# A two-layer decoder trunk on one core: the program's opening reordered, the attention bias read from a repeated distance table, the first norm weights spread by matmuls

## What is computed

```python
y = xf * lax.rsqrt(jnp.mean(xf * xf, axis=-1, keepdims=True) + EPS)
h = y * norm_mix[layer]                       # (256, 1024)
proj = h @ w_in[layer]                        # the first columns: q, k, v of the DeltaNet, then 4 + 4 for beta and alpha
# attention of group gi with dilation dil, for query qi and key kj of a block
dist = qi + C_BLOCK - kj
bias = table[t5_bucket(jnp.maximum(dist, 0) * dil)]      # 32 x 12 table, one column per head and group
s = jnp.einsum('brhnqd,brhnkd->brhnqk', qb, kb) * (D ** -0.5) + bias
s = jnp.where(valid, s, -jnp.inf)
```

## Time and profile before

| | |
|---|---|
| runs | median 2117.56 us of 3 (2116.93 to 2118.57) |
| profiled execution | 2120.26 us, its span 2118.5 us |
| granted TensorE clock, mean over the span | 0.987 |
| busy share of the span | PE 96%, PEld 82%, DVE 76%, ACT 58%, POOL 1% |
| moved by DMA | 517 MB, 244 GB/s over the span |

### The profile page before, as it was taken

How to read it: one execution, slowest core, us unless ns; L and a number is a source line. 1 busy time by engine, 2 the same in 40 slices (tenths; PEclk the granted TensorE clock), 3 DMA queues, 4 the chain that set the end, 5 groups by cost and what they waited for, 6 DMA issues and landing times.

```text
span 2118.5 us, 28922 instructions
## 1 busy us (share of the span) xinstructions
PE 2027.8 (96%) x10759; PEld 1728.0 (82%) x10759; DVE 1609.6 (76%) x1256; ACT 1233.7 (58%) x1013; POOL 16.5 (1%) x22
## 2 busy tenths in 40 slices
PE   7999999989997999999979999999999999999997
PEld 6998888879997988888868878888887888888885
DVE  5878865755445878955766888898888889888985
ACT  4544455444433554455446777777777777777774
POOL 0000000000000000000000000000000000000000
PEclk9999999999999999999988999999999999999999
DMA  8523455245554522455247999999999999999994
GB/s 279 160 80 100 140 178 179 89 151 188 179 190 136 177 82 90 145 164 186 91 149 260 387 344 378 359 362 368 353 379 341 382 358 364 375 341 372 351 375 179
DMA packets 240481, 516.97 MB, mean 244 GB/s; under 512 B 11519, under 2 KB 34167, under 8 KB 240412
## 3 DMA queue, kind: packets, MB, share of 16 engines
q1 hardware_dynamic: 238124, 507.60, 68.1%
q0 software_dynamic: 2288, 8.41, 1.1%
HBM read 513.86 MB, written 2.12 MB: 244 GB/s over the span
## 4 chain that ended last, share of the span: by engine, by line
PE 87%; DVE 7%; ACT 3%; issue 2%; DMA 0%; SPq 0%; DVEq 0%; ACTq 0%
PE PS L476 25%; PE PS L478 25%; PE PS L477 25%; PE PS L547 7%; DVE lo L1533 2%; ACT hi L1102 2%; PE PS L1002 1%; PE PS L978 1%; PE PS L496 1%; PE PS L758 0%; DVE a_act L1634 0%; DMA rows<-in_knorm_c 0%; PE PS L948 0%; PE PS L789 0%; DVE t_n L1556 0%
## 5 line engine op out<-in xcount | busy, mean ns | idle before, releaser
L1533 DVE TENSOR_TENSOR lo<-raw,hi 128x2048 fp32r<-128x2048 f32 x481 | 1095.0, 2290 | 295.0 <-ACT hi L1102 292.3
L1102 ACT ACTIVATE hi<-raw 128x2048 fp32r<-128x2048 f32 x481 | 919.6, 1915 | 337.8 <-PE PS L478 330.5
L476 PE MATMUL PS<-hi,e_hi 128*128 128x512 f32 x896 | 355.3, 397 | 1.4 <-DVE e_lo L1556 1.4
L478 PE MATMUL PS<-hi,e_lo 128*128 128x512 f32 x896 | 350.2, 391 | 0.0
L477 PE MATMUL PS<-lo,e_hi 128*128 128x512 f32 x896 | 350.2, 391 | 0.0
L476 PE MATMUL PS<-hi,actT_hi 128*128 128x512 f32 x640 | 253.9, 397 | 4.6 <-DVE lo L1533 4.1
L478 PE MATMUL PS<-hi,actT_lo 128*128 128x512 f32 x640 | 249.6, 390 | 0.0
L477 PE MATMUL PS<-lo,actT_hi 128*128 128x512 f32 x640 | 249.1, 389 | 0.0
L476 PE MATMUL PS<-hi,fT_hi 128*128 128x512 f32 x536 | 210.6, 393 | 9.8 <-DVE fT_lo L1556 9.3
L477 PE MATMUL PS<-lo,fT_hi 128*128 128x512 f32 x536 | 209.5, 391 | 0.0
L478 PE MATMUL PS<-hi,fT_lo 128*128 128x512 f32 x536 | 209.3, 390 | 0.0
(11 more groups left out here) (323 smaller groups left out, 2153.8 us busy)
## 6 DMA issues: line engine op xcount, KB each, us to landing
raw<-in_moe_w SPq DMA_DIRECT2D x336, 1024.0 KB, 5.8
raw<-in_w_in SPq DMA_DIRECT2D x92, 1024.0 KB, 5.2
raw<-in_ffn_w SPq DMA_DIRECT2D x33, 1024.0 KB, 5.3
raw<-in_w_br SPq DMA_DIRECT2D x12, 1024.0 KB, 5.0
raw<-in_w_out SPq DMA_DIRECT2D x8, 1024.0 KB, 5.2
hankel<-hankel_dram POOLq DMA_DIRECT2D x1, 1536.0 KB, 13.6
x<-in_x SPq DMA_DIRECT2D x2, 512.0 KB, 4.0
gain<-in_norm_mix POOLq DMA_DIRECT2D x2, 512.0 KB, 5.8
```

What stands on the lines that cost most here:

```text
L476: pe.matmul(out, a_hi, b_hi, start=first, stop=False, skip_group_check=True)
L478: return pe.matmul(out, a_lo, b_hi, start=False, stop=last, skip_group_check=True)
L1102: act.activation(hi[prog.u % SPLIT][:, :], raw[slot][:, :], COPY).then_inc(hi_made.sem, 1)
L1533: dve.tensor_tensor(lo[prog.u % RAW][:, :], raw[prog.u % RAW][:, :], hi[s][:, :].bitcast(F32), ALU.subtract).then_inc(lo_made.sem, 1)
```

## The change

It has these parts.

- **SP and ACT queues.** SP issues one row of `norm_mix` (4 KB) to partition 0 of `gain`, x in two halves with a semaphore each, the identity alone, and the first two weight units; then the narrow weights, the two parameters, the other ten mask tiles, and the rest of the weights. The bucket table, the bias table and the six rows are issued by ACT as its first instructions. POOL's load of `gain` for layer 0 is gone.
- **PE's opening.** 22 matmuls of a tile of ones with itself (into PSUM bank 7, read by nobody), then two matmuls of a row of ones with the norm row, which put the norm weights on 128 partitions in PSUM; DVE's first norm reads them there. Then the transposes of the normed input. The bias table's matmuls, the transpose of the rows and eight more matmuls of ones stand behind those transposes in `parameters`.
- **First unit ahead of the narrow product.** In both layers PE waits for the second `actT_lo` only, runs the first unit of `group_T`, then waits for the fourth, runs `narrow_product` and the second unit. In layer 0 the first unit holds after two of its four column tiles until ACT has copied `by_dist` and the rows out of PSUM.
- **ACT and DVE.** In layer 0 `prep(1)` stands ahead of `turn_input` on both, then `parameters` (ACT), a `prep`, the split of the narrow weights, a `prep`, and the small parameter work.
- **The bias.** POOL writes `by_dist` in three DMAs (one per group, 4 partitions each), 128 copies of each head's row, 2.36 MB in all, waits for them, and reads `bias` directly from DRAM: partition p starts at entry 127 − p of its own copy (row step 383), so nothing has to be flipped. ACT waits for the writes before it overwrites `by_dist` with b_q. The flip matrix, `hankel`, `spread_bias` and `bias_copies` are gone; DVE waits for `bias` at the attention.

```diff
# PE
-            pe.wait_ge(actT_lo_made.sem, actT_lo_made.at(L, idx + 3))
...
+        pe.wait_ge(tiny_made.sem, 5)
+        for _ in range(22):
+            mm(PS[:, 7, 0:P], ones, ones)
+
+        pe.wait_ge(first_row_here.sem, 16)
+        for half in range(2):
+            ins = mm(PS[:, half, :], ones_t[0:1, :], gain[0:1, half * 512:(half + 1) * 512])
+        ins.then_inc(gain_spread.sem, 1)
+
+        def parameters():
+
+            pe.wait_ge(picks_here.sem, 16)
+            pe.wait_ge(table_here.sem, 17)
+            for g in range(GROUPS):
+                ins = pe.matmul(PS[0:H, 1 + g, 0:DIST], table[:, g * H:(g + 1) * H], picks[:, g, :],
+                                start=True, stop=True)
+            ins.then_inc(by_dist_done.sem, 1)
+            pe.wait_ge(rows_here.sem, 16 * N_ROW_LOADS)
+            pe.transpose(PS[:, 3, DIST:DIST + R_N], rows[0:R_N, :], ident[0:R_N, 0:R_N]).then_inc(by_dist_done.sem, 1)
+            for _ in range(8):
+                mm(PS[:, 0, 0:P], ones, ones)
...
         def mixer(L):
+            if L == 0:
+                pe.wait_ge(ident_here.sem, 16)
             pe.wait_ge(norm_made.sem, norm_made.at(L, 1))
             turn_input(lambda t, k: hn[:, t, k * P:(k + 1) * P], 0, L)
+            if L == 0:
+                parameters()
+            pe.wait_ge(actT_lo_made.sem, actT_lo_made.at(L, 1))
+            group_T(0, (0,), hold=L == 0)
+            pe.wait_ge(actT_lo_made.sem, actT_lo_made.at(L, 3))
             pe.wait_ge(ab_split.sem, 2)
-            narrow_product(5, L)
...
+            narrow_product(7, L)
+            group_T(0, (1,))
+            if L == 0:
+                pe.wait_ge(by_dist_kept.sem, 2)
+            turn_narrow(4, L).then_inc(ab_done.sem, 1)
+            group_T(1)
+            pe.wait_ge(a_raw.sem, a_raw.at(L, 1))
+            group_T(0)
# ACT
+        load(picks[:, :, :], dram["buckets"], picks_here)
+        load(table[0:BUCKETS, :], dram["rel_bias"], table_here)
...
+        def parameters():
+
+            act.wait_ge(by_dist_done.sem, 2)
+            act.activation(by_dist[:, :, :], PS[0:H, 1:1 + GROUPS, 0:DIST], COPY).then_inc(by_dist_kept.sem, 1)
+            act.activation(small[:, :], PS[:, 3, DIST:DIST + R_N], COPY).then_inc(by_dist_kept.sem, 1)
+            act.wait_ge(par_here.sem, 32)
+            act.activation(a_rate[:, :, :], a_par[:, 0, :, :], EXP).then_inc(a_rate_e.sem, 1)
...
+            if L == 0:
+                prep(1)
             turn_input(0, L)
             if L == 0:
-                prep(3)
-            narrow_kept(5, L)
+                parameters()
+                prep(1)
+                split_narrow()
+                prep(1)
+                act.wait_ge(lb_m.sem, 1)
+                act.activation(lb[:, 4:6, :], lb[:, 4:6, :], EXP).then_inc(lb_e.sem, 1)
+            narrow_kept(7, L)
...
             used(L, 10)
+            if L == 0:
+                act.wait_ge(by_dist_out.sem, 16 * GROUPS)
# DVE
+            if L == 0 and phase == 0:
+                g = PS[:, 0:2, :].rearrange("p a b -> p (a b)")
             dve.wait_ge(norm_r.sem, norm_r.at(L, phase))
-            dve.wait_ge(gain_here.sem, 16 * (2 * L + phase + 1))
+            dve.wait_ge(*((gain_here.sem, 16 * (2 * L + phase)) if L or phase else (gain_spread.sem, 1)))
# POOL
-        pool.dma_start(gain[:, :], dram["norm_mix"][0:1, :].partition_broadcast(P)
-                       .rearrange("q o d -> q (o d)")).then_inc(gain_here.sem, 16)
         pool.wait_ge(by_dist_kept.sem, 1)
-        pool.dma_start(hankel_dram.rearrange("(g h) z -> h g z", g=GROUPS), by_dist[:, :, :])\
-            .then_inc(by_dist_out.sem, 16)
-        pool.wait_ge(by_dist_out.sem, 16)
-
-        pool.dma_start(hankel[:, :, :], bass.AP(hankel_dram.tensor, 0, [[1, P], [DIST, GROUPS * H], [1, T]]))\
-            .then_inc(hankel_here.sem, 16)
+        for g in range(GROUPS):
+            pool.dma_start(by_dist_dram[g * H:(g + 1) * H, :, :],
+                           by_dist[:, g, :].unsqueeze(1).broadcast_to([H, P, DIST])).then_inc(by_dist_out.sem, 16)
+        pool.wait_ge(by_dist_out.sem, 16 * GROUPS)
+
+        pool.dma_start(bias[:, :, :], bass.AP(by_dist_dram.tensor, P - 1,
+                                              [[DIST - 1, P], [P * DIST, GROUPS * H], [1, T]]))\
+            .then_inc(bias_here.sem, 16)
# SP
+        load(gain[0:1, :], dram["norm_mix"][0:1, :], first_row_here)
         for t in range(TT):
-            load(x[:, t, :], xr[t], x_here)
...
+            load(x[:, t, :], xr[t], x_here[t])
+        load(consts[:, K_ID, :], dram["masks"][:, K_ID, :], ident_here)
+        cols(0, C_QKV)
```

More of the change, by code:

```diff
@@ L285, in build @@
     dve_step = signal("dve_step")
-    x_here = signal("x_here")
-    consts_here = signal("consts_here")
+    x_here = [signal(f"x_here{t}") for t in range(TT)]
+    ident_here = signal("ident_here")
+    masks_here = signal("masks_here")
+    first_row_here = signal("first_row_here")
+    gain_spread = signal("gain_spread")
+    picks_here = signal("picks_here")
     rows_here = signal("rows_here")
@@ L498, in turn_input, with group_T @@
                 ins.then_inc(turned.sem, 1)
-            pe.wait_ge(actT_lo_made.sem, actT_lo_made.at(L, idx + 3))
-        def group_T(pair):
-            for half in range(2):
+        def group_T(pair, halves=(0, 1), hold=False):
+            for half in halves:
                 w_hi, w_lo = unit_ready()
                 for ct in range(4):
+                    if hold and ct == 2:
+                        pe.wait_ge(by_dist_kept.sem, 2)
                     out = PS[:, 2 * pair + ct // 2, (ct % 2) * T:(ct % 2 + 1) * T]
@@ L1121, in norm_scale @@
             load_tables()
-            if L == 0 and phase == 0:
-                act.wait_ge(x_here.sem, 32)
-            else:
+            if L or phase:
                 act.wait_ge(x_made.sem, x_made.at(L if phase else L - 1, 1 if phase else 2))
@@ L1176, in conv_in @@
                                    PS[:, 2 * (g % 2) + b, :].rearrange("p (a b) -> p a b", a=2), COPY).then_inc(a_raw.sem, 1)
-            def bias_copies(L, first):
-                if L == 0:
-                    for n in range(first, first + 3):
-                        act.wait_ge(bias_done.sem, n + 1)
-                        act.activation(bias[:, 2 * n:2 * n + 2, :].rearrange("p a b -> p (a b)"),
-                                       PS[:, 4 + n % 3, :], COPY).then_inc(bias_kept.sem, 1)
             def conv_tanh(g):
@@ L1614, in mixer @@
                 prep(1)
+            if L == 0:
+                prep(1)
             turn_input(0, L)
             if L == 0:
-                prep(3)
+                prep(1)
+                split_narrow()
+                prep(1)
             dve.memset(a_in[:, :, 0:3], 0.0).then_inc(pad_made.sem, 1)
             dve.wait_ge(pad_made.sem, L + 1)
+            if L == 0:
+                parameters()
+                dve.wait_ge(masks_here.sem, 16)
             def conv(g):
@@ L1624, in conv @@
                 if g == 0 and L == 0:
-                    dve.wait_ge(rows_kept.sem, 1)
+                    dve.wait_ge(by_dist_kept.sem, 2)
                 for tap in range(TAPS):
@@ L1950, in mix_turned @@
                                          v.bitcast(F32), ALU.mult, ALU.subtract).then_inc(actT_lo_made.sem, 1)
+            if L == 0:
+                dve.wait_ge(bias_here.sem, 16)
             scaled(0)
@@ L2290, in _ @@
                  .rearrange("q o l h -> q (o l) h"), par_here)
+        load(consts[:, K_ID + 1:K_N, :], dram["masks"][:, K_ID + 1:K_N, :], masks_here)
         def mixer(L):
-            for g in range(3):
+            for g in range(0 if L else 1, 3):
                 cols(L, C_QKV + g * W)
```

139 lines of the change are left out of this document (58 added, 81 removed).

## The result

The changed kernel takes 2183.49 us (median of 4 runs, 2182.87 to 2188.43), the kernel before, on the same chip, 2118.07. The ratio is 1.0313, 95% interval [1.0299, 1.0328]. I forecast 2111.8 and a range up to 2116.9; the result lies outside it, on the side to which I gave 0.05.

A forecast was written before the change was run, and what follows sets the result against it. PE was taken to bound the chain (87%). Opening 1.4, flips 3.1 and order 1.3 summed to 5.8 us, taken off the median of 2117.56 for 2111.8, range 2108.3 to 2116.9.

The forecast's parts named there:

- Loads: DMA queues: weight units land ahead of their splits, and POOL's 2.36 MB repeated table costs nothing.
- Rival 3: Weight loads: the repeated table, on four engines for 26 us, starves them; PE loses 12 us, 2123.8; chance 0.05.
- E: Point after layer 0's second weight unit where the narrow output is turned; forecast at 34.7 instead of 36.14, 1.4 us earlier.
- Flips: Layer 0's mixer: removing the flip matmuls from PE's path gains 3.1 us, ends 2.6 and 5.2.
- Order: Layer 1: narrow product behind the first half unit ends PE's wait for the fourth actT_lo; gain 1.3 us, ends 0 and 1.4.
- Opening: Layer 0's start: warm-ups, gain by matmul and parameters behind the transposes; first unit at 20.3, gain 1.4 us.
- Rival 1: Opening: the dummies do not raise the clock; 3.5 us late, 0.9 left over, 2116.7; chance 0.17.
- Rival 2: Opening: the clock stays up from the dummies on, transposes in 1.8 us; sum 7.6, 2110.0; chance 0.15.
- Rival 4: Opening: transposes do not raise the clock, parameters take 8.0 for 4.0 us; sum 1.8, 2115.8; chance 0.06.

The follow-up runs named there:

- one_at_a_time: Changed kernel with POOL waiting for each repeated write before issuing the next; 2159.0 us, one run.
- dram_copy: Changed kernel with by_dist written once to DRAM (18 KB) and the three repeated writes reading that copy; 2115.8 us, one run.
- spread128: Changed kernel with by_dist on 128 partitions, 32 to a head, each writing 4 of the 128 copies; 2116.12 us, ratio 0.9993 to the kernel before.
- flips_only: Kernel before without flip matmuls and bias copies, bias made by the writes of spread128; 2116.05 us against 2119.03, ratio 0.9987.
- order_layer1: Kernel before with the first weight unit ahead of the narrow product in layer 1 alone; 2118.57 us, ratio 1.0000.
- step32: As spread128, but each write reads only partitions 0, 32, 64, 96, each 128 times; 2138.83 us, one run.
- step36: As spread128, but each write reads only partitions 0, 36, 72, 108, each 128 times; 2121.01 us, one run.
- no_warm: spread128 without the 22 warm-up matmuls ahead of the gain's; 2112.70 us, ratio 0.9979 to the kernel before.
- opening3: no_warm with 1 dummy matmul instead of 8 behind the parameters; 2113.96 us, ratio 0.9977 to the kernel before.

## Why the prediction was wrong

**The failed step** is the part "Loads": "I cost it at nothing". I asked who waits for the repeated table, found nobody, and took the DMA share of 0.77, an average over sixteen engines, as its cover. What counted was what it does to the transfers beside it. Rival 3 had the mechanism: a few engines, a unit complete only with its slowest. Its price was a rate of 22.5 GB/s an engine from POOL's queue before, and most of those bytes go to 128 partitions. The runs showed 23.3 GB/s for all engines of the three writes together: 101 us, where I had 26. A rate per engine was carried over to a source that gave 23.3 GB/s to all its engines together. I also let only four engines be slow. That three writes at once spread the trouble is shown by one_at_a_time: engine time of the queue 68.3% against 22.0%. So the loss was not 12 us at most, but 65. The Trainium skill's rule that I named there (DMA: Bandwidth & Descriptors, Rules for kernel authors), on an outermost dimension under 16, agrees with the 22.0% of one_at_a_time, 3.5 engines' worth for a write with a dimension of four. It says how many engines are held and not for how long, and alone it does no harm: dram_copy has that shape and loses nothing that shows.

The prices, by source, with all else nearly equal (the times of the second to fourth row are of one run each):
| source of the writes | writes, us | PE waits for lo to 170 us | time |
|---|---|---|---|
| partitions 0 to 3 (after) | 101.2 | 64.6 | 2183.49 |
| 0, 32, 64, 96 | 57.1 | 19.2 | 2138.83 |
| 0, 36, 72, 108 | 36.6 | 2.0 | 2121.01 |
| DRAM | 20.5 | 1.5 | 2115.8 |
| 128 partitions | 14.3 | 1.5 | 2116.12 |

With three writes at once the lead of the weight units absorbs some 37 us of them: 101.2 − 64.6 = 36.6, 57.1 − 19.2 = 37.9. The time of the third row is not the price of its writes. Its E is 39.95, 4.3 later than in spread128, where nothing but the pace of PE differs up to there:
```profile
17.13 4.20 PE L566 MATMUL PS<-picks,wide_table 33*128 33x384 f32 x6
```
These table matmuls took 2.20 us in spread128.

**Flips, 3.1 us: right.** flips_only shows 62.91 turned into 59.87 and 3.0 us in the median (interval about 1 to 5).

**Order, 1.3 us: nearly right, in layer 1.** 1.1 in order_layer1. In the kernel after, from the timeline of PE in layer 1:
```profile
723.28 3.68 PE L493 MATMUL PS<-consts,hn 128*128 128x128 f32 x16 [9.31 <-DVE hn L1595]
...
741.61 0.29 PE L584 MATMUL PS<-consts,narrow 8*128 8x8 f32 x2
```
18.33 against 19.28, 0.95 gained.

**Opening, 1.4 us: the mechanism right, the size gone.** Timeline of the kernel after:
```profile
1.83 7.84 PE L545 MATMUL PS<-ones_t 128*128 128x128 f32 x44 [1.83 <-DVE ones_t L1585]
9.60 1.98 PE L545 MATMUL PS<-gain,ones_t 1*128 1x512 f32 x4
11.70 2.47 DVE L1595 SCALAR_TENSOR_TENSOR hn<-x,stat,PS 128x1024 f32<-128x1024 f32 x2 [9.79 <-PE PS L545]
14.31 3.58 PE L493 MATMUL PS<-consts,hn 128*128 128x128 f32 x16 [2.73 <-DVE hn L1595]
21.72 0.36 PE L473 MATMUL PS<-actT_hi,hi 128*128 128x256 f32 x1
36.19 0.28 PE L584 MATMUL PS<-consts,narrow 8*128 8x8 f32 x2
```
The warm-ups end at 9.67 instead of 8.2, because their passes stand 0.22 apart at first, 26 of them in 5.7 us; the pace doubled only near 7.5, where I had let it rise after 3.2 us, as in layer 1. The gain is spread at 11.6 instead of 10.0, hn at 14.2 instead of 12.5. From there the sum holds: transposes 3.58 at the lower clock (3.57 forecast), parameters 3.9 (4.0), two units and the narrow product 36.19 − 21.72 = 14.47 (14.43). E is where it was before, 36.14, so all of the 1.4 went into the late doubling of the pace. The first weights landed near 10.4 where I had 9, and PE did not wait for them: the lo of unit 0 was made by 16.4.

**Rival 1** falls: the pace did rise. **Rival 2** falls: the transposes ran at the lower level. **Rival 4** falls in this profile: parameters took 3.9 us, at the higher level, right behind 3.58 us of transposes. But luck had a part in that. Five more profiles have this opening of PE; in spread128, step32 and dram_copy the pace rose as here, near 17 to 18 us, while in step36 and one_at_a_time it rose only near 26.4, the table's matmuls took 4.20 and 4.00 us, and E came at 39.95 and 39.98. That is rival 4 in two profiles of six, where I gave it 0.06. **Rival 3** is the one that came true, in mechanism and not in price.

Without the slow reads, the change is worth 2.2 us by the medians (spread128) where I had 5.8, and its interval, 3.4 us less to 0.6 more, does not leave out zero. The parts make 4: 3.0 from the flips, 1 from the order in layer 1, nothing from the opening. The profile agrees with them: layer 1's first DeltaNet transposes come at 732.54 in spread128 and at 736.95 before, 4.4 earlier. Why the median is lower stays open. That profile is of a run of 2114.95, while the ten runs reach up to 2121.28; a late rise of the pace in some of them would fit, and is not shown. Without the warm-ups as well (no_warm) it is 6.3 us under the kernel before by the medians (2119.03 in that comparison), 4.4 by the ratio; its E is 33.09, 3.1 ahead of that of the kernel after, and its span 2.7 under that of spread128.

**Open:** what sets the 36.6 us of four ports (dram_copy, with the same shapes and no port, takes 20.5, so the shape may have a part); what decides when the pace of PE rises in the opening; whether a layout with by_dist outside b_q's place would free ScalarE from its wait; and whether reading an 18 KB table with a falling step over partitions would make the 128 copies needless. The last two were not tried.

## What to carry to other kernels

Before costing a transfer at nothing because nobody waits for it, look at where its source lies and how many engines it holds: a repeated read of a few neighbouring SBUF partitions moved 23 GB/s, and the weights queued behind its packets for 65 us. A rate per engine is good only for transfers with the same spread over partitions. Spread the source over all 128 partitions, and issue one such transfer at a time if it can't be spread: that took the waits for weights from 64.6 to 6.6 us here, though others may then wait for the transfer itself. And work that only warms an engine belongs behind, not ahead of, the result that the next engine waits for: the gain was spread at 6.9 instead of 11.6.

## What was not expected of the hardware

- A packet of 4.6 KB from partitions 0 to 3 held a DMA engine for 2.0 us while eleven engines were held so, against 0.16 us for the average packet (3.7 KB) of the same queue before. The weights' packets, 0.09 us each once served, were 89 in those 25 us instead of 2055.
- The clock column is no guide to the first microseconds of an opening. It reads 1.00 in windows of the kernel after in which 128-column passes stand 0.22 apart, and all through opening3's first 23 us, where the pace visibly doubles at 23.0. The traces' first records of the clock stand at 7.45 us in the kernel after and at 23.06 in opening3, just where the pace doubles; ahead of its first record a trace has nothing to take off, and the column shows 1.00. There the spacing of the passes is the reading. A window of the kernel after, then two of opening3 (19 passes in 3.8 us, then 27 in 3.0, at the same 1.00).
```profile
1.80:7.50 5.70, 5.67 (x26) 5.67 (x27) 0.07 (x1) 2.43 (x3) 0.00 (x0) 1.00 0.93 309
```
```profile
19.20:23.00 3.80, 3.80 (x19) 3.80 (x19) 0.57 (x1) 3.79 (x6) 2.35 (x3) 1.00 1.04 398
23.00:26.00 3.00, 3.00 (x27) 3.00 (x26) 3.00 (x3) 1.45 (x1) 0.11 (x1) 1.00 1.06 397
```
- no_warm and opening3 are the same program up to the table matmuls, and the same six passes took 2.20 us in one profile and 4.21 in the other, right behind sixteen transposes at the lower pace (on two chips). step36 and spread128, the same up to there and on one chip, show the same, 4.20 and 2.20 us. So a rise of the clock there is not sure from one execution to the next, and a single profile can be off by some 4 us in the opening.
